# Between two layers of a decoder: weights rounded and turned in another order, two subtractions on GpSimd

## The chip, the cores and the metric

The kernel runs on one core of a Trainium2 chip. The metric is the device time of one execution in microseconds. Five engines work side by side: TensorE (PE; its weight loads are PEld), VectorE (DVE), ScalarE (ACT), GpSimd (POOL) and SyncE (SP), which here issues all DMAs. Each takes its own instructions in order and waits for others by semaphores.

## The reference, cut to what matters

256 tokens of width 1024 go through two layers, all in float32. Layer 0 is an HGRN2 mixer, layer 1 differential attention with one shared K/V; behind each mixer stands a grouped top-2 mixture of 16 experts. Each half of a layer ends in a residual sum and a normalisation:

```python
for l in range(DEPTH):                      # DEPTH = 2
    mix = hgrn2_mixer(x, ...) if l == 0 else diff_attention(x, k_sh, v_sh, ...)
    x = layer_norm(DEEPNORM_ALPHA * x + mix, ln1_g[l], ln1_b[l])
    ffn = moe_ffn(x, router_w, router_b, moe_w_gate[l], moe_w_up[l], moe_w_down[l])
    x = layer_norm(DEEPNORM_ALPHA * x + ffn, ln2_g[l], ln2_b[l])
```

Layer 1 begins with `x @ kv_w` and `x @ w_q`. The change lies between the end of the experts of layer 0 and these products.

## The kernel before, in words

**Products in three parts.** Activations and projection weights are split into a rounded high part and a low part (the rest). A projection is the sum of three products: high by high (number 0), the low part of x by the high weights (number 1), the high part of x by the low weights (number 2). The projection weights are cut into 36 pieces of 128 x 2048 (1 MB); `piece(i)` on TensorE multiplies one, in three groups of 16 products. `high(i)` on ScalarE (L805) rounds a piece into one of three buffers `w_hi`; `low(i)` on VectorE (L1185) subtracts that from the piece in place. `A_PIECES` is 20: pieces 0 to 19 belong to layer 0, piece 20 opens layer 1. The pieces lie in a ring of 12 places, which the expert weights use too; SyncE loads a place when the products that read it have ended. The buffers `w_hi` share memory with three of the four `spare` places of expert weights.

**Experts.** `moe(layer)` on each engine goes through 8 pairs of experts, two in each turn of a loop. In a pair TensorE multiplies gate (L2129), up (L2129), turns the hidden rows and multiplies down (L2143, L2160). ScalarE takes Silu (L1035), a copy of the hidden rows (L1039), and the output in two halves (`ys_hi`, L1052), of which VectorE takes the low part (L1667). After the last pair TensorE adds the outputs up (L2235) in four banks that hold the residual sum. An `overflow` part runs only if an expert has more tokens than its place holds; no instruction of it ran in the profiled execution. Behind it ScalarE loads the table with Ln and Exp (L1060), then runs `high(20)`.

**The passage between the layers.** VectorE takes the statistics of the four banks (L1674, L1214). ScalarE gives rstd by Ln (L859) and Exp (L862), VectorE refines it in small instructions (L1217 before, L1232 to L1236 after the root) and normalises token tile 0 (L1253), ScalarE tile 1 (L826), each in two halves. TensorE in the meantime multiplies zeros (`nothing`, L1850, 63 of them), then turns x by `turn_normed` (L1828 is the transpose) into four banks of PSUM: of a half, all four blocks of tile 0, then all of tile 1. From each bank the scaled and shifted x is written twice, rounded as `x_hi` and whole as `xT`: banks 0 and 2 by ScalarE (L819), 1 and 3 by VectorE (L1197); VectorE subtracts them into `x_lo` (L1728), and after each half it runs one `low`, of piece 20 or 21. Six more zero products of 256 columns (L2362) stand between the turns and piece 20. Piece 20 opens with the first product in two halves (L1895); all others come from L1906. `high(21)` follows ScalarE's part of this. GpSimd has nothing to do from its last weighing of gates (L756) to `affine` (L744), which scales and shifts the rows of x by two instructions of 128 x 2048.

**What sets the order.** It is written out by hand for each engine; nothing is planned at run time. A counting semaphore (`hi_ready`, `lo_ready`) says how many pieces are rounded and split; both are incremented in the order of the pieces.

Of the kernel before, what the change touches and what calls it, by code (L numbers as in the profile page):

```python
# [28 lines left out]
SLOTS = 64  # L29
# [62 lines left out]
def build(nc, ins, out):  # L92
    ctx = ExitStack()
    with ctx:
# [176 lines left out]
        o_gslot = sb("o_gslot", [P, 1])  # L271
        o_weights = [spare[:, c, :, :] for c in range(SPARE)] + late[1:3]

# [416 lines left out]
        def _(pool):  # L690
# [59 lines left out]
            for layer in range(LAYERS):  # L750
# [29 lines left out]

                if layer == 0:

                    pool.wait_ge(tp_ready, 4 * 2 + 4)
                    pool.wait_ge(kq_dve, 1)
                    affine()
# [8 lines left out]
        def _(act):  # L794
# [189 lines left out]
            def moe(layer):  # L984
                def overflow():
                    count = act.value_load(rounds[0:1, 0:1], min_val=1, max_val=ROUNDS)
                    with act.If(count > 1):
                        with act.Fori(1, count, 1):
                            act.wait_ge(orows_c_ps, done)
                            nc.scalar.activation(o_rows[:, 0:COLS], ps[:, BANK_C, :], ACT.Copy).then_inc(orows_act, 1)  # L990
                            act.wait_ge(oxc_ps, done)
                            for k in range(HALF_K):
# [16 lines left out]
                                                 scale=o_gslot[0:SLOTS, 0:1]).then_inc(oys_act, 1)  # L1009
                            act.reg_add(done, done, 1)  # L1010

                def take_xe(ready, value, bank, ks, cols):
# [17 lines left out]

                def experts(two, odd):
                    i = 2 * two + odd
                    pair = PAIRS * layer + i
                    act.wait_ge(gate_ps, 2 * pair + 2)
                    nc.scalar.activation(silu[:, :], ps[:, BANK_A, :], ACT.Silu).then_inc(silu_ready, 1)  # L1035
                    if not odd:
                        take_xe(xe_ps, gathered(layer, two, 0) + 1, BANK_C, (0, 1), slice(0, 4 * SLOTS))
                    act.wait_ge(ht_ps, pair + 1)
                    nc.scalar.activation(hT[:, :, :].rearrange("p j s -> p (j s)"), ps[:, BANK_A, :],  # L1039
                                         ACT.Copy).then_inc(ht_ready, 1)  # L1040
                    if not odd:
                        take_xe(xe_ps, gathered(layer, two, 0) + 2, BANK_B, (4, 5), slice(0, 4 * SLOTS))

                    act.wait_ge(put_ps, pair + 2)
                    nc.scalar.activation(silu[:, 0:T], ps[:, BANK_B if odd else BANK_A, 0:T], ACT.Copy,
                                         accum_out=gslot[:, 0:1]).then_inc(gslot_ready, 1)
                    for part, bank, ready in ((0, BANK_C, yc_ps), (1, BANK_D, yd_ps)):
                        act.wait_ge(ready, pair + 1)
                        if part == 0:
                            act.wait_ge(gslot_ready, pair + 1)  # L1050
                            act.wait_ge(seeded, TT * (layer + 1))
                        nc.scalar.activation(ys_hi[:, part * COLS:(part + 1) * COLS], ps[:, bank, :], ACT.Copy,  # L1052
                                             scale=gslot[:, 0:1]).then_inc(ys_act, 1)

                with act.Fori(0, PAIRS // 2, 1) as two:
                    experts(two, 0)
                    experts(two, 1)
                act.wait_ge(slots_ready, layer + 1)
                overflow()
                nc.scalar.preload_act_table_set(LOG_EXP)  # L1060
                if layer == 0:
                    high(A_PIECES)

# [23 lines left out]
            rounded_and_whole(2)  # L1087
            high(A_PIECES + 1)

# [79 lines left out]
        def _(dve):  # L1169
# [553 lines left out]
            for half in range(2):  # L1723
                rounded_and_whole(2 * half + 1)
                for ready, value in ((x_hi_ready, 5), (x_hi_dve, 5), (xT_act, 1), (xT_dve, 1)):
                    dve.wait_ge(ready, value + half)
                ks = slice(4 * half, 4 * half + 4)
                V.tensor_tensor(x_lo[:, ks, :], xT[:, ks, :], x_hi[:, ks, :].bitcast(F32), ALU.subtract  # L1728
                                ).then_inc(x_lo_ready, 1)
                low(20 + half)  # L1730

# [30 lines left out]
            def rms_of_sums(i, half, pairs):  # L1762
# [8 lines left out]
                step(rstd(i, values))  # L1771

            low(22)
            low(23)
# [48 lines left out]
        def _(pe):  # L1823
# [7 lines left out]
            def turn_normed():  # L1831
                for half in range(2):
                    for t in range(TT):
                        pe.wait_ge(x_half[t], half + 1)
                        for k in range(HALF_K * half, HALF_K * (half + 1)):
                            last = turn(x, t, k, TURN_BANKS[k // 2])
                            if t == 1 and k % 2:
                                last.then_inc(tp_ready, 1)

# [19 lines left out]
            def piece(i, after=()):  # L1859
# [15 lines left out]
                if (n, part) in ((AO1, 1), (BO1, 1)):  # L1875
# [6 lines left out]
                    return  # L1882
                for number, (w, xs) in enumerate(products):
                    if number == 1 and first_of_half:
# [422 lines left out]

            for _ in range(63):
                nothing(BANK_A, COLS // 4)
            turn_normed()  # L2310

# [48 lines left out]

            for _ in range(6):
                nothing(BANK_A, COLS // 2)  # L2362
            for i in range(20, 24):
# [40 lines left out]
```

## Time and profile before

| what | us |
|---|---|
| median of 3 runs (lowest, highest) | 700.84 (700.36, 702.13) |
| the profiled execution | 700.01 |
| its span, first to last instruction | 698.3 |
| TensorE busy in the span | 684.1 |
| VectorE, ScalarE, GpSimd busy | 307.1, 228.6, 52.8 |
| zero products between the layers begin | 354.60 |
| first turn of x, first product of piece 20 | 358.81, 361.18 |

Times inside the execution count from the first instruction. In the time-ordered views a row gives start, duration, engine, line of the kernel, operation, output and inputs, the count of instructions merged, and in brackets how long the engine had been idle before it and what released it. Two instructions of one engine can overlap by a tenth of a microsecond, since a record takes in the latency of its write.

### The profile page before, as it was taken

Reading aid. Unit: us, or ns where it says so; the run is one execution under the profiler, and the core shown is the slowest. Engines: PE = TensorE matmul, PEld = TensorE weight load, DVE = VectorE, ACT = ScalarE, POOL = GpSimd, SP = SyncE. Lnnn points to the kernel's source line nnn. Section 1 sums busy time; section 2 is a strip of 40 time slices with the busy share of each in tenths; the row PEclk is TensorE's granted clock in tenths of the full one; section 3 lists DMA queues with packets and bytes.
Section 4 is the critical chain, followed back from the end, with each engine's and each line's share of the span. In section 5 each row is a group of like instructions: output and inputs, shape, how many; then the busy total and the mean of one; then the engine's idle time right before and its main releaser. Section 6 shows DMA issues by size and latency. Waiting matters only on the chain.

```text
span 698.3 us, 13465 instructions
## 1 busy us (share of the span) xinstructions
PE 684.1 (98%) x5519; PEld 408.9 (59%) x5520; DVE 307.1 (44%) x563; ACT 228.6 (33%) x430; POOL 52.8 (8%) x57
## 2 busy tenths in 40 slices
PE   9999999999999999999999999999999999999993
PEld 8989988864335335335379987887433533533531
DVE  5689956686112012012076687678711111211205
ACT  4566567151112112012173656716111111211202
POOL 2035100010000000000004100001000000000001
PEclk9999999999999999999999999999999999999998
DMA  8999335989999999999999643498999999999991
GB/s 316 304 382 390 131 122 184 408 336 424 420 420 420 411 421 410 415 421 421 411 387 388 225 158 125 177 394 335 419 419 423 420 412 422 419 404 422 421 384 61
DMA packets 50870, 244.04 MB, mean 349 GB/s; under 512 B 6201, under 2 KB 6546, under 8 KB 26258
## 3 DMA queue, kind: packets, MB, share of 16 engines
q1 hardware_dynamic: 50834, 243.55, 87.3%
q8 instruction: 24, 0.39, 0.2%
q14 instruction: 12, 0.10, 0.0%
HBM read 242.49 MB, written 1.05 MB: 349 GB/s over the span
## 4 chain that ended last, share of the span: by engine, by line
PE 89%; DVE 7%; ACT 2%; issue 1%; ACTq 0%; DVEq 0%
PE ps L2129 32%; PE ps L1911 10%; PE ps L1906 10%; PE ps L2160 8%; PE ps L2143 8%; PE ps L2110 5%; PE ps L2091 4%; DVE ring_lo L1185 2%; PE ps L1878 2%; PE ps L1828 1%; PE ps L2099 1%; PE ps L2057 1%; PE ps L2197 1%; PE ps L1850 1%; DVE scratch L1343 1%
## 5 line engine op out<-in xcount | busy, mean ns | idle before, releaser
L2129 PE MATMUL ps<-weights,scratch 128*32 128x512 f32 (+1 forms) x1536 | 167.8, 592 | 0.0
L2129 PEld LDWEIGHTS ps<-weights,scratch 128*32 128x32 f32 x1536 | 49.9, 110 | 113.9 <-issue 113.9
L1185 DVE TENSOR_TENSOR ring_lo<-weights,w_hi 128x2048 fp32r<-128x2048 f32 x36 | 81.9, 2292 | 9.4 <-ACT w_hi L805 9.2
L1686 DVE TENSOR_TENSOR scratch<-ps,early 128x512 f32<-128x512 f32 x16 | 11.0, 689 | 168.1 <-PE ps L2129 168.1
L805 ACT ACTIVATE w_hi<-weights 128x2048 fp32r<-128x2048 f32 x35 | 66.6, 1914 | 22.9 <-PE ps L1911 11.5
L1667 DVE SCALAR_TENSOR_TENSOR rounded<-ps,gslot,rounded 128x512 fp32r<-128x512 f32 x32 | 24.0, 751 | 91.7 <-ACT rounded L1052 91.7
L2129 PE MATMUL ps<-tail,scratch 128*32 128x512 f32 (+1 forms) x512 | 56.4, 592 | 0.0
L1052 ACT ACTIVATE rounded<-ps,gslot 128x512 fp32r<-128x512 f32 x32 | 22.0, 688 | 88.4 <-PE ps L2160 47.0
L1017 ACT ACTIVATE scratch<-ps,ln_col 128x256 f32<-128x256 f32 (+1 forms) x40 | 19.3, 540 | 86.9 <-PE ps L2110 84.7
L1035 ACT ACTIVATE early<-ps 128x512 f32<-128x512 f32 x16 | 9.6, 597 | 98.7 <-PE ps L2129 98.7
L2129 PEld LDWEIGHTS ps<-tail,scratch 128*32 128x32 f32 x512 | 16.6, 110 | 38.3 <-issue 38.3
L1906 PE MATMUL ps<-x_lo,w_hi 128*128 128x256 f32 x256 | 33.8, 285 | 0.0
L756 POOL TENSOR_TENSOR early<-rounded,gate_of 128x256 f32<-128x256 f32 x14 | 8.6, 616 | 330.0 <-PE ps L2215 330.0
L1906 PE MATMUL ps<-x_hi,ring_lo 128*128 128x256 f32 x256 | 33.4, 283 | 0.0
L1639 DVE TENSOR_SCALAR scratch<-ps,ln_col 128x256 f32<-128x256 f32 (+1 forms) x40 | 18.7, 513 | 32.0 <-PE ps L2110 30.8
L2110 PE MATMUL ps<-rounded 128*128 128x256 f32 x128 | 32.2, 290 | 0.0
L1906 PEld LDWEIGHTS ps<-x_lo,w_hi 128*128 128x128 f32 x256 | 31.8, 191 | 0.5 <-issue 0.3
L1906 PEld LDWEIGHTS ps<-x_hi,ring_lo 128*128 128x128 f32 x256 | 31.8, 192 | 0.2 <-DVE ring_lo L1185 0.2
L2091 PE MATMUL ps<-rounded,early_r 128*128 128x512 f32 x112 | 31.5, 411 | 0.0
L2110 PE MATMUL ps<-rounded,x_lo 128*128 128x256 f32 x128 | 31.3, 283 | 0.0
L2160 PE MATMUL ps<-places,scratch 128*32 128x512 f32 (+1 forms) x256 | 30.6, 595 | 0.0
L2160 PE MATMUL ps<-weights,scratch 128*32 128x512 f32 (+1 forms) x256 | 30.4, 592 | 0.0
(293 smaller groups left out, 991.2 us busy)
## 6 DMA issues: line engine op xcount, KB each, us to landing
weights<-in_moe_w_gate SPq DMA_DIRECT2D x64, 1024.0 KB, 12.6
weights<-in_moe_w_up SPq DMA_DIRECT2D x32, 1024.0 KB, 11.5
places<-in_moe_w_down SPq DMA_DIRECT2D x32, 1024.0 KB, 11.1
tail<-in_moe_w_up SPq DMA_DIRECT2D x32, 1024.0 KB, 16.6
weights<-in_moe_w_down SPq DMA_DIRECT2D x32, 1024.0 KB, 11.2
weights<-in_a_w_in SPq DMA_DIRECT2D x15, 1024.0 KB, 12.9
weights<-in_kv_w SPq DMA_DIRECT2D x8, 1024.0 KB, 15.6
weights<-in_a_w_out SPq DMA_DIRECT2D x4, 1024.0 KB, 15.2
```

Of the source, the lines that this page charges most:

```text
L805: nc.scalar.activation(w_hi[:, i % HI, :, :].rearrange("p k n -> p (k n)"), ring[:, piece_slot(i), :, :].rearrange("p k n -> p (k n)"), AC ...
L1017: last = nc.scalar.activation(xe[:, k, cols], ps[:, bank, j * width:(j + 1) * width], ACT.Identity, scale=ln_col(2 * layer, 0, k), bias=ln ...
L1052: nc.scalar.activation(ys_hi[:, part * COLS:(part + 1) * COLS], ps[:, bank, :], ACT.Copy, scale=gslot[:, 0:1]).then_inc(ys_act, 1)
L1185: V.tensor_tensor(low_part(i), ring[:, piece_slot(i), :, :], w_hi[:, i % HI, :, :].bitcast(F32), ALU.subtract).then_inc(lo_ready, 1)
L1667: V.scalar_tensor_tensor(ys_lo[:, cols], ps[:, (BANK_C, BANK_D)[part], :], gslot[:, 0:1], ys_hi[:, cols].bitcast(F32), ALU.mult, ALU.subtr ...
L1906: last = mm(ps[:, bank, c * T:(c + 1) * T], w[:, k, first:first + P], xs[:, HALF_K * part + k, :], start=opens and c == 0 and k == 0, stop ...
L1911: last = mm(ps[:, bank, :], xs[:, HALF_K * part + k, j * P:(j + 1) * P], w[:, k, :], start=opens and k == 0, stop=closes and k == HALF_K - ...
L2091: last = mm(ps[:, 2 * t + j, :], put[:, t * P:(t + 1) * P], part[:, j * COLS:(j + 1) * COLS], start=False, stop=True, skip_group_check=True)
L2110: last = mm(ps[:, banks[j // 2], first:first + 4 * SLOTS], part[:, t, k * P:(k + 1) * P], pick[:, t, :, :].rearrange("p e s -> p (e s)"), ...
L2129: last = mm(ps[rows, bank, :], own[:, HALF_K * part + k, rows], w, start=part == 0 and k == 0, stop=part == 1 and k == HALF_K - 1)
L2143: last = mm(ps[rows, bank, :], hT[:, 2 * part + k, rows], w, start=part == 0 and k == 0, stop=part == 1 and k == 1)
L2160: last = mm(ps[rows, bank, :], hT[:, 2 * part + k, rows], w, start=part == 0 and k == 0, stop=part == 1 and k == 1)
```

## The change

In the experts' loop the last two pairs are written out behind it on ScalarE. The table with Ln and Exp is loaded right behind the last Silu, in both layers; in the overflow part the Silu table is loaded before and the other one after. In layer 0 `high(20)` stands between the two halves of the last pair's `ys_hi`, and `high(21)` behind the overflow part. The low parts of pieces 20 and 21 are made by GpSimd, behind its last weighing; VectorE's two are gone, and it waits for both before `low(22)`. The weights of the overflow part move to places that don't share memory with the buffers in use. `turn_normed` turns both tiles of a bank before it goes to the next. Piece 20 multiplies in the order 0, 2, 1. The 63 zero products of 128 columns become 40, with 29 of 64 columns behind them, and the six of 256 columns are gone.

```diff
--- before.py
+++ after.py
@@ -269,7 +269,7 @@
         o_hT = at(hid_place + F, FT, SLOTS)
         o_put = at(hid_place + F + FT * SLOTS, T)
         o_gslot = sb("o_gslot", [P, 1])
-        o_weights = [spare[:, c, :, :] for c in range(SPARE)] + late[1:3]
+        o_weights = [spare[:, c, :, :] for c in range(1, SPARE, 2)] + late[1:5]
 
         def o_weight(matrix, part):
             return o_weights[2 * matrix + part]
@@ -779,6 +779,10 @@
                 weigh(PAIRS // 2 - 1, 1)
 
                 if layer == 0:
+                    for i in range(A_PIECES, A_PIECES + 2):
+                        pool.wait_ge(hi_ready, i + 1)
+                        pool.tensor_tensor(low_part(i), ring[:, piece_slot(i), :, :], w_hi[:, i % HI, :, :].bitcast(F32),
+                                           ALU.subtract).then_inc(lo_ready, 1)
 
                     pool.wait_ge(tp_ready, 4 * 2 + 4)
                     pool.wait_ge(kq_dve, 1)
@@ -985,6 +989,7 @@
                 def overflow():
                     count = act.value_load(rounds[0:1, 0:1], min_val=1, max_val=ROUNDS)
                     with act.If(count > 1):
+                        nc.scalar.preload_act_table(ACT.Silu)
                         with act.Fori(1, count, 1):
                             act.wait_ge(orows_c_ps, done)
                             nc.scalar.activation(o_rows[:, 0:COLS], ps[:, BANK_C, :], ACT.Copy).then_inc(orows_act, 1)
@@ -1008,6 +1013,7 @@
                             nc.scalar.activation(o_ys[0:SLOTS, :], ps[0:SLOTS, BANK_A, :], ACT.Copy,
                                                  scale=o_gslot[0:SLOTS, 0:1]).then_inc(oys_act, 1)
                             act.reg_add(done, done, 1)
+                        nc.scalar.preload_act_table_set(LOG_EXP)
 
                 def take_xe(ready, value, bank, ks, cols):
 
@@ -1028,11 +1034,13 @@
                 take_xe(xc_ps, layer + 1, BANK_C, range(0, 4), columns_of(0))
                 nc.scalar.preload_act_table(ACT.Silu)
 
-                def experts(two, odd):
+                def experts(two, odd, last_pair=False):
                     i = 2 * two + odd
                     pair = PAIRS * layer + i
                     act.wait_ge(gate_ps, 2 * pair + 2)
                     nc.scalar.activation(silu[:, :], ps[:, BANK_A, :], ACT.Silu).then_inc(silu_ready, 1)
+                    if last_pair:
+                        nc.scalar.preload_act_table_set(LOG_EXP)
                     if not odd:
                         take_xe(xe_ps, gathered(layer, two, 0) + 1, BANK_C, (0, 1), slice(0, 4 * SLOTS))
                     act.wait_ge(ht_ps, pair + 1)
@@ -1051,15 +1059,18 @@
                             act.wait_ge(seeded, TT * (layer + 1))
                         nc.scalar.activation(ys_hi[:, part * COLS:(part + 1) * COLS], ps[:, bank, :], ACT.Copy,
                                              scale=gslot[:, 0:1]).then_inc(ys_act, 1)
-
-                with act.Fori(0, PAIRS // 2, 1) as two:
+                        if last_pair and part == layer == 0:
+                            high(A_PIECES)
+
+                with act.Fori(0, PAIRS // 2 - 1, 1) as two:
                     experts(two, 0)
                     experts(two, 1)
+                experts(PAIRS // 2 - 1, 0)
+                experts(PAIRS // 2 - 1, 1, last_pair=True)
                 act.wait_ge(slots_ready, layer + 1)
                 overflow()
-                nc.scalar.preload_act_table_set(LOG_EXP)
                 if layer == 0:
-                    high(A_PIECES)
+                    high(A_PIECES + 1)
 
             def second_parts(layer):
                 act.wait_ge(parts_ps, TT * layer + 2)
@@ -1085,7 +1096,6 @@
             normalise(1)
             rounded_and_whole(0)
             rounded_and_whole(2)
-            high(A_PIECES + 1)
 
             def take_kq(n):
                 dst = qT if n in (BQ0, BQ1) else kT
@@ -1727,7 +1737,6 @@
                 ks = slice(4 * half, 4 * half + 4)
                 V.tensor_tensor(x_lo[:, ks, :], xT[:, ks, :], x_hi[:, ks, :].bitcast(F32), ALU.subtract
                                 ).then_inc(x_lo_ready, 1)
-                low(20 + half)
 
             def take_kq(n):
                 dst = qT if n in (BQ0, BQ1) else kT
@@ -1770,6 +1779,7 @@
                 V.scalar_tensor_tensor(values(0), squares, 1.0 / P, low_end, ALU.mult, ALU.add).then_inc(var_ready, 1)
                 step(rstd(i, values))
 
+            dve.wait_ge(lo_ready, A_PIECES + 2)
             low(22)
             low(23)
             take_kq(K0)
@@ -1829,13 +1839,12 @@
                                            src[:, t, k * P:(k + 1) * P], ident[:, :])
 
             def turn_normed():
-                for half in range(2):
+                for pair in range(HALF_K):
                     for t in range(TT):
-                        pe.wait_ge(x_half[t], half + 1)
-                        for k in range(HALF_K * half, HALF_K * (half + 1)):
-                            last = turn(x, t, k, TURN_BANKS[k // 2])
-                            if t == 1 and k % 2:
-                                last.then_inc(tp_ready, 1)
+                        pe.wait_ge(x_half[t], pair // 2 + 1)
+                        for k in (2 * pair, 2 * pair + 1):
+                            last = turn(x, t, k, TURN_BANKS[pair])
+                    last.then_inc(tp_ready, 1)
 
             def turn_half(half, value):
                 for t in range(TT):
@@ -1880,7 +1889,8 @@
                         if number == 2 and k == HALF_K - 1:
                             last.then_inc(proj_ready, 1)
                     return
-                for number, (w, xs) in enumerate(products):
+                for number in (0, 2, 1) if i == A_PIECES else range(3):
+                    w, xs = products[number]
                     if number == 1 and first_of_half:
                         pe.wait_ge(x_lo_ready, 2 * call + part + 1)
                     if number == 2:
@@ -2305,8 +2315,10 @@
 
 
 
-            for _ in range(63):
+            for _ in range(40):
                 nothing(BANK_A, COLS // 4)
+            for _ in range(29):
+                mm(ps[:, BANK_A, 0:SLOTS], zeros16[:, :], zeros16[:, 0:SLOTS], start=True, stop=True)
             turn_normed()
 
             def attention_scores(h):
@@ -2358,8 +2370,6 @@
                         attention_out(h)
                 return between
 
-            for _ in range(6):
-                nothing(BANK_A, COLS // 2)
             for i in range(20, 24):
                 piece(i)
             piece(24, (attend(0),))
```

## Rows read from the trace of the kernel before

**Rows 1.** Page, part 1: busy us, share of the span, instructions

```profile
PE 684.1 (98%) x5519; PEld 408.9 (59%) x5520; DVE 307.1 (44%) x563; ACT 228.6 (33%) x430; POOL 52.8 (8%) x57
```

**Rows 2.** TensorE in order of time: start, us, what

```profile
354.60 3.75 PE L1850 MATMUL ps<-zeros 128*128 128x128 bf16 x63 [0.21 <-issue]
358.81 1.97 PE L1828 MATMUL ps<-ident,x_sb 128*128 128x128 f32 x16 [0.46 <-DVE x_sb L1253]
360.61 0.82 PE L1850 MATMUL ps<-zeros 128*128 128x256 bf16 x6
361.18 2.15 PE L1895 MATMUL ps<-x_hi,w_hi 128*128 128x256 f32 x16
...
367.46 2.08 PE L1906 MATMUL ps<-x_hi,w_hi 128*128 128x256 f32 x16
369.38 2.08 PE L1906 MATMUL ps<-x_lo,w_hi 128*128 128x256 f32 x16
...
684.55 2.40 PE L2235 MATMUL ps<-rounded,early_r 128*128 128x512 f32 x8
```

**Rows 3.** ScalarE in order of time, same stretch

```profile
348.69 0.69 ACT L1052 ACTIVATE rounded<-ps,gslot 128x512 fp32r<-128x512 f32 x1 [3.13 <-PE ps L2160]
...
353.49 1.28 ACT L1060 ACT_TABLE_LOAD   x1 [0.67 <-issue]
...
356.60 0.28 ACT L859 ACTIVATE rs<-mv,eps 128x2 f32<-128x2 f32 x1
...
359.72 1.02 ACT L819 ACTIVATE x_hi<-ps,pcol 128x256 fp32r<-128x256 f32 x2 [0.34 <-PE ps L1828]
```

**Rows 4.** VectorE in order of time, same stretch

```profile
356.03 0.28 DVE L1214 BATCH_NORM_AGGREGATE mv<-stats 128x2 f32<-128x12 f32 x2
...
357.22 0.35 DVE L1232 SCALAR_TENSOR_TENSOR rs<-rs 128x1 f32<-128x1 f32 x2 [0.70 <-ACT rs L862]
...
357.94 1.53 DVE L1253 TENSOR_SCALAR x_sb<-ps,mv,rs 128x512 f32<-128x512 f32 x2
...
361.97 1.23 DVE L1728 TENSOR_TENSOR x_lo<-xT,x_hi 128x1024 fp32r<-128x1024 f32 x1
...
375.70 2.29 DVE L1185 TENSOR_TENSOR ring_lo<-weights,w_hi 128x2048 fp32r<-128x2048 f32 x1
```

**Rows 5.** GpSimd in order of time, whole span

```profile
52.63 2.02 POOL L738 TENSOR_TENSOR scratch<-scratch 128x512 f32<-128x512 f32 x1 [11.66 <-ACT scratch L927]
...
65.97 1.30 POOL L738 TENSOR_TENSOR scratch<-scratch 128x512 f32<-128x512 f32 x1 [2.95 <-ACT scratch L927]
...
375.92 11.25 POOL L744 TENSOR_TENSOR x_sb<-x_sb,scratch 128x2048 f32<-128x2048 f32 x2 [53.61 <-DVE scratch L1190]
474.38 2.68 POOL L769 TENSOR_SCALAR scratch<-x_sb,mv,rs 128x512 f32<-128x512 f32 x1 [87.21 <-DVE rs L1236]
484.92 0.62 POOL L763 TENSOR_TENSOR early<-rounded,gate 128x256 f32<-128x256 f32 x1 [7.86 <-DVE scratch L1639]
```

**Rows 6.** VectorE in order of time, beside GpSimd and alone

```profile
53.59 1.60 DVE L1341 TENSOR_TENSOR scratch<-scratch 128x512 f32<-128x512 f32 x1
...
70.69 0.69 DVE L1341 TENSOR_TENSOR scratch<-scratch 128x512 f32<-128x512 f32 x1
...
485.08 0.47 DVE L1579 CAST second<-rg 1x7 int32<-1x7 f32 x1
```

**Rows 7.** DMA issues near 329.5 and 332, last column us to landing

```profile
weights<-in_kv_w SPq DMA_DIRECT2D x1, 1024.0 KB, 18.2
...
weights<-in_kv_w SPq DMA_DIRECT2D x1, 1024.0 KB, 20.5
```

**Rows 8.** TensorE in order of time, small bf16 products in layer 1

```profile
478.44 0.18 PE L2065 MATMUL ps<-both,later 128*128 128x16 bf16 x1
...
478.56 0.17 PE L2069 MATMUL ps<-both,ones 128*128 128x16 bf16 x1
```

**Rows 9.** Windows: stretch, length, busy times, granted clock, DMA share, GB/s

```profile
691.90:692.10 0.20, 0.00 (x0) 0.00 (x0) 0.20 (x1) 0.00 (x0) 0.20 (x1) 0.75 0.00 0
```

## What the change does to the time: the prediction

> **What bounds the kernel now.** I read the page first, then the chain of waits, which in the passage between the two layers runs through ScalarE's `high(20)` and logarithm, VectorE's small instructions and L1253 to the turns, then that stretch engine by engine in order of time, and last the places where GpSimd and VectorE read SBUF together. TensorE is busy for 684.1 of 698.3 us [rows 1], so every microsecond that it loses or wins between the layers moves the end; none of its waits is for a DMA, and the expert loops of the second layer are issued against its progress, so they shift with it. The passage is this. TensorE ends the experts and plays 63 zero products from 354.60; the last is over near 358.35. It then stands 0.46 us until VectorE has written the first normalised half, turns x at 358.81, plays six zero products at 360.61, and starts piece 20 at 361.18 [rows 2]. A group of sixteen products is followed by the next after 1.92 us (367.46 to 369.38), and a piece has three groups, 5.76 us; but piece 20 takes 6.28, from 361.18 to 367.46: its second group waits for x_lo, done at 363.20 (L1728, 361.97 and 1.23 [rows 4]), its third for the low part that VectorE makes behind that.
>
> What comes before the first turn is the normalisation's small work. The variance is there at 356.31 (356.03 and 0.28) [rows 4], but ScalarE is in `high(20)`, and the logarithm starts at 356.60 [rows 3]. The first of VectorE's five small instructions starts at 357.22, and L1253 follows at 357.94 [rows 4]: 0.72 us from first to next. The first turn starts 0.87 us behind L1253.
>
> **The change part by part.** The sum is against the profiled execution, 700.01 us (span 698.3); the median of the three runs is 0.83 higher, 700.84.
>
> *Rounding and table on ScalarE.* The table load (1.28 us at 353.49 [rows 3]) goes behind the last Silu, in front of ScalarE's wait for the up products and the turned hidden rows: no cost. In layer 1 it stood before a wait for VectorE anyway: no gain. `high(20)` goes behind ScalarE's first half of the last outputs, which ends at 349.38; its weights were issued at 329.53 and took 18.2 us, so they are there at 347.7 [rows 3, 7]. It runs to about 351.3, and the second half still starts at 352.13. `high(21)` takes the table load's place: its load is issued by 332.4 and lands 20.5 us later, 352.9 at the latest [rows 7]; it runs from 353.5 to 355.4. So the logarithm follows the variance at once, near 356.35 instead of 356.60: -0.24 us, if nothing else is late. The peeled pair costs some straight-line code beside long waits, which I take as nothing.
>
> *Turns and zero products.* Turning bank by bank lets ScalarE start after 4 turns instead of 6, 0.24 us earlier (16 turns run 1.80 us, 0.11 each, from 358.81 to 360.61 [rows 2]). That matters only because the six zero products go: ScalarE's x_hi (359.72 and 1.02 [rows 3]) is ready 1.93 us after the first turn, with the change 1.69, and the turns last 1.80. The first product then follows the turns directly: -0.57 us (361.18 less 360.61). The filler ahead: 40 products of 128 columns at 57 ns (3.75 us less one 0.22 latency, over 62) are 2.3 us. For 29 of 64 columns there is no row; five of 16 columns follow each other at about 28 ns (478.44 to 478.56 for the first and fifth [rows 8]), 128 columns at 57; so 0.8 to 1.7 us, and I take 0.9, nearer the small ones. The filler then ends by 357.9, at worst at 358.6, when the first turn could not start sooner than 358.57: nothing to 0.1 us.
>
> *Order (0, 2, 1) and the low parts on GpSimd.* Piece 20 no longer waits for VectorE's low part, and x_lo, ready 4.4 us after the first turn (361.97 and 1.23 against 358.81 [rows 2, 4]), is asked for 5.6 us after it (1.80 and two groups of 1.92). Both stalls go: 6.28 less 5.76, -0.52 us. VectorE is freed of two subtractions of 2.29 us (the length of L1185 [rows 4]), which no later product waits for. Together, from the first turn on: 0.57 + 0.52 = 1.09 us won.
>
> *What GpSimd does to VectorE.* This is where the change turns round. GpSimd takes 9.2 us for two instructions of the same size (375.92 and 11.25 give 387.17; it could not begin before VectorE's L1185, 375.70 and 2.29, was over at 377.99) [rows 4, 5]: 4.6 us each. From 65.97 one of 512 elements takes 1.30, four times that is 5.2, the upper bound; I take 4.6, the same shape. `low(20)` starts 0.1 us behind `high(20)`, at 351.4, and ends at 356.0. `low(21)` has its input since 355.4 and follows: 356.05 to 360.65. Ready in time for TensorE, both. But while a two-input GpSimd instruction runs, a VectorE instruction that reads two tensors in SBUF stands still. L1341 takes 1.60 us at 53.59 and 0.69 at 70.69; it ends at 55.19, half a microsecond after GpSimd's L738 (52.63 and 2.02, so 54.65) [rows 5, 6]. Size doesn't save it: a cast of 1x7 at 485.08 takes 0.47 us and ends at 485.55, where GpSimd's L763 (484.92 and 0.62) ends at 485.54 [rows 5, 6]. L1232, L1234, L1235 and L1236 read two SBUF tensors each, and the first of them would be issued at 357.0, a microsecond into `low(21)`. It stands until 360.65. The chain to L1253 is 0.72 us from there, or 0.57 since the standing instruction's own start is over; L1253 starts at about 361.3 instead of 357.94: +3.36 us. This takes in the 0.24 that ScalarE had won. Queued behind L1232 on VectorE is all of the normalisation, ScalarE's half of it, and with them the turns, so TensorE, too. L1217 (before L1232, one input) may be held as well: up to +0.25.
>
> Sum: 3.36 - 1.09 = +2.27 us, 702.3 against 700.01, or 703.1 against the median.
>
> [...]
>
> **The rivals.**
> A. *GpSimd's reads don't hold these small instructions.* For it: L769 holds nothing, and no row shows a 128x1 operand under a two-input GpSimd instruction. Against it: the 1x7 cast. Then all the gains stand: 0.24 + 1.09 = 1.33 us, 698.7 in the profile, 699.5 by the median, not slower. The same comes if `low(21)` starts only after L1236, that is later than about 357.7; it would need the second weights to land 3 us later than the bound above. It decides at one point: whether GpSimd is in a two-input instruction when L1232 is issued.
> B. *The held time also costs the clock.* TensorE stands from 357.9 to 362.2, 4.3 us. At the end of the span its last product ends at 686.95 (684.55 and 2.40 [rows 2]) and the granted clock goes from 1.00 to 0.50, to 1.2 GHz, at 692.0 (0.75 in 691.9 to 692.1 [rows 9]), 5.05 us later. So 4.3 us is a little short of what that drop took. If it falls here, at least the turns take twice their 1.80 us, and perhaps the first group of products, 1.92, too: 1.8 to 3.7 more. Total +4.1 to +6.0: 704.9 to 706.8.
> C. *GpSimd is slower for this output type* (it never writes rounded values before). At the bound of 5.2 us each `low(21)` ends at 361.85: +1.2, so 704.3.
>
> **How the numbers follow.** Held, clock kept, GpSimd at 4.6: 0.62, time 703.1, own range 702.7 to 703.7. Held and slower (C): 0.08. Held and clock lost (B): 0.16. Not held (A): 0.14. The range from 701.2 to 705.6 leaves out A and the far end of B. A measurement tells 0.3%, 2.1 us, from no change. The forecast of +2.3 lies just over it: of the 0.70 in the held cases at full clock about 0.17 falls within 2.1, with nearly all of A the chance of no difference is 0.29; slower 0.67; faster 0.04.
>
> **What would show it.** VectorE's L1232 between the layers lasts about 3.7 us and ends with GpSimd's second subtraction; ScalarE's logarithm starts near 356.35; TensorE's first turn starts near 362.2, its first piece 1.8 us later, pieces 20 and 21 take 5.76 us each without a stall. A first turn before 359, with GpSimd at work beside it, would prove the main step wrong; a granted clock of 0.50 behind the wait would show B; GpSimd's subtractions longer than 4.8 us would show C.

## The result and the profile after

The change makes the kernel slower: 704.20 us median (703.57 to 705.62, 7 runs) against 700.84 (7 runs beside it). The ratio is 1.0053, with a 95% interval of 1.0044 to 1.0062. The profiled execution took 704.20 us with a span of 702.5; that is 4.2 us more span than before. The forecast was slower, 703.1.

In the kernel after, lines stand lower: L1850 is now L1859 (its 64-column form L2321), L1828 is L1838, L1895 and L1906 are L1905 and L1916, L1217 is L1227, L1232 is L1242, L1253 is L1263. The kernels of the experiments shift them again by a few lines: L1217 is L1229 in e1 and e11, L1232 in e7, L1233 in e12.

TensorE of the kernel after, in order of time, answers to [rows 2]:

```profile
354.50 2.47 PE L1859 MATMUL ps<-zeros 128*128 128x128 bf16 x40 [0.21 <-issue]
356.81 1.01 PE L2321 MATMUL ps<-zeros 128*128 128x64 bf16 x29
361.86 3.68 PE L1838 MATMUL ps<-ident,x_sb 128*128 128x128 f32 x16 [4.04 <-DVE x_sb L1263]
365.19 3.22 PE L1905 MATMUL ps<-x_hi,w_hi 128*128 128x256 f32 x16
368.24 2.08 PE L1916 MATMUL ps<-x_hi,ring_lo 128*128 128x256 f32 x16
...
372.08 2.08 PE L1916 MATMUL ps<-x_hi,w_hi 128*128 128x256 f32 x16
...
688.75 2.40 PE L2245 MATMUL ps<-rounded,early_r 128*128 128x512 f32 x8
```

The first turn waits 4.04 us, and sixteen turns then last 3.33 us until the next group instead of 1.80. VectorE, the same stretch ([rows 4]):

```profile
355.94 0.28 DVE L1224 BATCH_NORM_AGGREGATE mv<-stats 128x2 f32<-128x12 f32 x2
356.25 3.98 DVE L1227 TENSOR_SCALAR rs<-mv 128x2 f32<-128x2 f32 x1
360.26 0.35 DVE L1242 SCALAR_TENSOR_TENSOR rs<-rs 128x1 f32<-128x1 f32 x2
...
360.99 1.53 DVE L1263 TENSOR_SCALAR x_sb<-ps,mv,rs 128x512 f32<-128x512 f32 x2
```

GpSimd and ScalarE, the same stretch, each in order of time ([rows 3] has ScalarE's before):

```profile
351.16 9.04 POOL L784 TENSOR_TENSOR ring_lo<-weights,w_hi 128x2048 fp32r<-128x2048 f32 x2 [28.95 <-ACT w_hi L809]
```

```profile
353.05 1.92 ACT L809 ACTIVATE w_hi<-weights 128x2048 fp32r<-128x2048 f32 x1 [0.33 <-issue]
356.25 0.29 ACT L863 ACTIVATE rs<-mv,eps 128x2 f32<-128x2 f32 x1 [1.29 <-DVE mv L1224]
```

An instruction on two numbers per partition takes 3.98 us, and ends (360.23) with GpSimd's second subtraction (351.16 + 9.04 = 360.20). The windows of the kernel after have the granted clock in the third column from the right:

```profile
358.00:360.00 2.00, 0.00 (x0) 0.00 (x0) 2.00 (x1) 0.00 (x0) 2.00 (x1) 1.00 1.07 391
360.00:362.00 2.00, 0.14 (x1) 0.14 (x2) 1.90 (x8) 1.01 (x2) 0.20 (x1) 0.69 1.04 384
362.00:364.00 2.00, 2.00 (x10) 2.00 (x11) 0.65 (x2) 1.43 (x4) 0.00 (x0) 0.50 1.05 385
364.00:366.00 2.00, 2.00 (x12) 2.00 (x11) 1.87 (x5) 2.00 (x6) 0.00 (x0) 0.50 1.06 393
366.00:368.00 2.00, 2.00 (x12) 2.00 (x12) 2.00 (x4) 2.00 (x3) 0.00 (x0) 0.60 1.04 408
368.00:372.00 4.00, 4.00 (x36) 4.00 (x35) 3.87 (x5) 0.57 (x1) 0.00 (x0) 1.00 1.04 389
```

TensorE has been idle since 357.82. A mean of 0.69 over two microseconds puts the step from 1.00 to 0.50 (2.4 to 1.2 GHz) at 360.8, and 0.60 puts the step back at 367.6. The turns and most of the first group of products ran at half clock.

**Where the 4.2 us are.** I count from the start of the zero products, since that is the same work in every kernel: so what a profiled execution gains or loses ahead of the passage drops out (the zeros start anywhere from 354.50 to 356.54 in the kernels below).

| us from the start of the zeros | before | after | e1 | e2 |
|---|---|---|---|---|
| first turn | 4.21 | 7.36 | 3.98 | 7.37 |
| first turn to first product | 2.37 | 3.33 | 1.86 | 1.86 |
| piece 20 | 6.28 | 6.89 | 5.82 | 5.82 |
| in all: piece 21 begins | 12.86 | 17.58 | 11.66 | 15.05 |

e1 is the change without the hold (`low(21)` later), e2 the change with the hold but with TensorE kept busy. So the edits that were to gain give 12.86 - 11.66 = 1.20; the hold costs 15.05 - 11.66 = 3.39; the lost clock costs 17.58 - 15.05 = 2.53. Together +4.72. The passage begins 0.10 earlier (354.50 against 354.60), so piece 21 begins 4.62 later; 0.4 us come back at 441, where a wait of TensorE is gone (below), and the last group of products starts 4.20 later, at 688.75 instead of 684.55.

### The profile page after: what moved, and what is told of

Read it like the earlier page. It is cut to its first block, busy times and chain, and to the rows that moved or that the text cites. A ratio compares the mean times of both kernels' runs of the same rounds, so it can differ in the third digit from the quotient of the medians.

```text
span 702.5 us, 13451 instructions
## 1 busy us (share of the span) xinstructions
PE 685.1 (98%) x5519; PEld 410.5 (58%) x5520; DVE 310.0 (44%) x561; ACT 228.8 (33%) x430; POOL 62.0 (9%) x59
## 4 chain that ended last, share of the span: by engine, by line
PE 95%; DVE 3%; ACT 1%; issue 0%; DVEq 0%; ACTq 0%
PE ps L2139 31%; PE ps L1921 14%; PE ps L1916 13%; PE ps L2170 8%; PE ps L2153 8%; PE ps L2120 5%; PE ps L2101 4%; PE ps L1887 2%; PE ps L1838 1%; PE ps L2109 1%; PE ps L2067 1%; PE ps L2207 1%; PE ps L1859 1%; PE ps L1905 1%; DVE stats L1684 1%; DVE rs L1227 1%
## 5 line engine op out<-in xcount | busy, mean ns | idle before, releaser
L1916 PE MATMUL ps<-x_lo,w_hi 128*128 128x256 f32 x256 | 33.7, 284 | 0.0
L1916 PE MATMUL ps<-x_hi,ring_lo 128*128 128x256 f32 x256 | 33.3, 283 | 0.0
L1916 PEld LDWEIGHTS ps<-x_lo,w_hi 128*128 128x128 f32 x256 | 31.8, 191 | 0.3 <-issue 0.3
L1916 PEld LDWEIGHTS ps<-x_hi,ring_lo 128*128 128x128 f32 x256 | 31.9, 192 | 0.0
```

The source lines that it names most:

```text
L1916: last = mm(ps[:, bank, c * T:(c + 1) * T], w[:, k, first:first + P], xs[:, HALF_K * part + k, :], start=opens and c == 0 and k == 0, stop ...
```

## The experiments

All ratios are against the kernel before, run on the same chip. Most differences are small against 700 us, so the column "piece 21 begins", counted from the zeros as above, is read first and the time second. It comes from one profiled execution of each kernel; e1, e9, e10 and e13, which do the same work there, agree in it within 0.01, as do before and e5.

| kernel | median us (runs) | ratio, 95% interval | piece 21 begins, us |
|---|---|---|---|
| e1_after_stat | 698.62 (7) | 0.9973, 0.9962 to 0.9984 | 11.66 |
| e2_long_filler | 703.04 (6) | 1.0033, 1.0021 to 1.0045 | 15.05 |
| e3_lows_on_vector | 700.39 (10) | 0.9998, 0.9988 to 1.0007 | 12.65 |
| e5_no_six_zeros | 700.74 (10) | 1.0003, 0.9994 to 1.0012 | 12.87 |
| e6_order_012 | 700.62 (10) | 1.0000, 0.9990 to 1.0009 | 12.87 |
| e8_six_zeros_back | 699.88 (10) | 0.9986, 0.9977 to 0.9995 | 12.20 |
| e9_table_back | 699.52 (10) | 0.9982, 0.9973 to 0.9992 | 11.66 |
| e7_one_input | 706.45 (2) | 1.0080, 1.0061 to 1.0098 | 17.78 |
| e11_behind_l1217 | 706.39 (4) | 1.0072, 1.0055 to 1.0089 | 17.20 |
| e12_one_input_l1232 | 704.75 (2) | 1.0051, 1.0031 to 1.0072 | 16.33 |
| e10_vector_code | 698.99 (11) | 0.9973, 0.9964 to 0.9982 | 11.67 |
| e13_one_memset | 700.13 (10) | 0.9978, 0.9968 to 0.9988 | 11.66 |

**e1_after_stat.** `low(21)` on GpSimd starts only when VectorE's small instructions are over.

```diff
+                        if i > A_PIECES:
+                            pool.wait_ge(ln_stat, 2)
```

> The changed kernel with one wait more: GpSimd starts its subtraction for piece 21 only when VectorE has finished the statistics (ln_stat 2). Theory (VectorE is held by GpSimd's two-input instruction, and the wait that follows costs TensorE its clock): both go, the first turn starts near 358.5 instead of 361.86, piece 20 starts 1.8 us later, the clock stays at 1.00; 1.3 us faster than the kernel before, ratio 0.998. Rival (the loss comes from the filler, the peeled pair on ScalarE or the order of turns): the first turn stays near 361.9 and the time near 704.

Measured: 698.62, and the interval of the ratio excludes 1. TensorE, VectorE and GpSimd of this kernel, each in order of time:

```profile
354.64 2.41 PE L1861 MATMUL ps<-zeros 128*128 128x128 bf16 x40 [0.21 <-issue]
...
358.62 1.97 PE L1840 MATMUL ps<-ident,x_sb 128*128 128x128 f32 x16 [0.73 <-DVE x_sb L1265]
360.48 2.14 PE L1907 MATMUL ps<-x_hi,w_hi 128*128 128x256 f32 x16
...
366.30 2.08 PE L1918 MATMUL ps<-x_hi,w_hi 128*128 128x256 f32 x16
```

```profile
356.40 0.17 DVE L1229 TENSOR_SCALAR rs<-mv 128x2 f32<-128x2 f32 x1
357.03 0.35 DVE L1244 SCALAR_TENSOR_TENSOR rs<-rs 128x1 f32<-128x1 f32 x2 [0.46 <-ACT rs L868]
...
361.79 1.72 DVE L1740 TENSOR_TENSOR x_lo<-xT,x_hi 128x1024 fp32r<-128x1024 f32 x1
```

```profile
351.31 4.57 POOL L786 TENSOR_TENSOR ring_lo<-weights,w_hi 128x2048 fp32r<-128x2048 f32 x1 [28.96 <-ACT w_hi L811]
357.86 4.57 POOL L786 TENSOR_TENSOR ring_lo<-weights,w_hi 128x2048 fp32r<-128x2048 f32 x1 [1.98 <-DVE rs L1248]
```

The same 128x2 instruction takes 0.17 us when GpSimd is idle beside it, against 3.98. One wait moves the kernel from slower to faster, so the hold, with the clock that it costs, is the whole loss. `x_lo` now meets `low(21)` and is held 0.5 us (1.72 against 1.23 [rows 4]), which in the order 0, 2, 1 nobody waits for. VectorE's four L1209 behind L1265, which read PSUM, keep their length beside it (0.99 to 1.00 us for two, as L1207 in the changed kernel without it). This version is faster than both kernels.

**e2_long_filler.** 66 more zero products, to fill the held time.

```diff
-            for _ in range(40):
+            for _ in range(106):
```

> The changed kernel with 106 instead of 40 zero products of 128 columns, so that TensorE is busy until about 361.6 while VectorE is held. Theory (hold and clock are two costs): the hold stays, first turn near 361.9, but the clock stays at 1.00 and 2.6 us come back: about +2.0 us against the kernel before (702.8), 1.4 to 2.7 faster than the changed kernel. Rival (the slow turns and first products come from something else than the idle time): no gain, near 704.2.

TensorE of this kernel, and one window with its granted clock:

```profile
354.81 6.15 PE L1859 MATMUL ps<-zeros 128*128 128x128 bf16 x106 [0.20 <-issue]
360.80 1.01 PE L2321 MATMUL ps<-zeros 128*128 128x64 bf16 x29
362.18 1.97 PE L1838 MATMUL ps<-ident,x_sb 128*128 128x128 f32 x16 [0.38 <-DVE x_sb L1263]
364.04 2.14 PE L1905 MATMUL ps<-x_hi,w_hi 128*128 128x256 f32 x16
...
369.86 2.08 PE L1916 MATMUL ps<-x_hi,w_hi 128*128 128x256 f32 x16
```

```profile
361.00:364.00 3.00, 2.62 (x44) 2.41 (x40) 2.46 (x7) 2.57 (x5) 0.00 (x0) 1.00 1.05 388
```

The hold stays (first turn at 7.37 as at 7.36), the clock does not fall, and 2.53 us of the passage go. In the medians it is less: 704.20 less 703.04 is 1.2 us, the ratios differ by 0.0020 and their intervals just touch; of e2 the profiled execution (702.18) is the fastest of six. The mean granted clock of the whole execution says that the clock is lost in every run of the change: 0.990 to 0.992 in its seven, 0.993 to 0.995 in the six of e2. How many microseconds of it other executions pay, no trace shows.

**e3_lows_on_vector.** The GpSimd part undone: both low parts back on VectorE, order 0, 1, 2 again; the rest of the change stays.

```diff
-                    for i in range(A_PIECES, A_PIECES + 2):
-                        pool.wait_ge(hi_ready, i + 1)
-                        pool.tensor_tensor(low_part(i), ...)
...
+                low(20 + half)
...
-                for number in (0, 2, 1) if i == A_PIECES else range(3):
+                for number in range(3):
```

> The changed kernel with GpSimd's part alone undone: the low parts of pieces 20 and 21 are VectorE's again, after each half of x_lo, and piece 20 multiplies in the order 0, 1, 2. Theory: no hold and no lost clock; the logarithm is 0.24 us earlier and the zero products are gone, but piece 20 then stands longer for x_lo and its low part, which are ready only 0.24 us earlier than before: -0.3 us against the kernel before. Rival (the six zero products cost their full 0.57 us wherever VectorE stands): -0.8 us.

Measured: no change in the time, and 0.21 in the passage. TensorE has this:

```profile
359.33 1.97 PE L1834 MATMUL ps<-ident,x_sb 128*128 128x128 f32 x16 [0.67 <-DVE x_sb L1259]
361.19 2.15 PE L1901 MATMUL ps<-x_hi,w_hi 128*128 128x256 f32 x16
363.78 2.18 PE L1912 MATMUL ps<-x_lo,w_hi 128*128 128x256 f32 x16 [0.44 <-DVE x_lo L1734]
```

The product starts right behind the turns, and then its half microsecond is spent again in front of x_lo. What remains is the earlier logarithm.

**e5_no_six_zeros.** The kernel before, without the six zero products alone.

```diff
-            for _ in range(6):
-                nothing(BANK_A, COLS // 2)
```

> The kernel before with nothing but the six zero products of 256 columns left out. Theory: piece 20 starts 0.4 us earlier (x_hi ready at 360.74), but its third group still waits for VectorE's low part at 365.4: no change, within 0.1 us. Rival: the time falls by 0.4 to 0.6 us.

Measured: nothing, 12.87 against 12.86. The first product starts 2.08 us after the first turn instead of 2.37; the gain is lost at x_lo, for which TensorE stands 0.22 us. The six zeros of the kernel before stood where TensorE would have waited anyway.

**e6_order_012** and **e8_six_zeros_back.** e1 with the old order, and e1 with the six zeros.

```diff
-                for number in (0, 2, 1) if i == A_PIECES else range(3):
+                for number in range(3):
```

```diff
+            for _ in range(6):
+                nothing(BANK_A, COLS // 2)
```

> e1_after_stat with piece 20 in the order 0, 1, 2. Theory: its second group then waits for x_lo, ready 4.9 us after the first turn (GpSimd holds it half a microsecond) and asked for 3.8 after it: +1.1 us, near 699.7. Rival (x_lo is never late): no change.

> e1_after_stat with the six zero products of 256 columns put back between the turns and piece 20. Theory (piece 20 is now bound by TensorE alone): they cost their 0.57 us in full, 699.2, where leaving them out of the kernel before brought nothing. Rival (something else holds piece 20): no change against e1_after_stat.

TensorE and VectorE of e6:

```profile
360.88 2.14 PE L1907 MATMUL ps<-x_hi,w_hi 128*128 128x256 f32 x16
363.99 2.18 PE L1918 MATMUL ps<-x_lo,w_hi 128*128 128x256 f32 x16 [0.96 <-DVE x_lo L1740]
```

```profile
362.19 1.74 DVE L1740 TENSOR_TENSOR x_lo<-xT,x_hi 128x1024 fp32r<-128x1024 f32 x1
```

In the old order TensorE waits 0.96 us for an x_lo that GpSimd holds; 12.87 less 11.66 is 1.21, all that e1 gains. Half a microsecond of this is the hold of x_lo, so it is the price of the old order beside GpSimd and not of the order alone. In e8 the six zeros cost 12.20 - 11.66 = 0.54. The order with GpSimd's low parts pays even with the six zeros in place (piece 20 takes 5.84 us in e8, from 361.75 to 367.59, for 6.28); dropping the zeros pays only with these two (e5, e3). The new order with VectorE's low parts was not run.

**e9_table_back.** e1 with the table load behind the overflow part, where it was.

```diff
-                    if last_pair:
-                        nc.scalar.preload_act_table_set(LOG_EXP)
...
                 overflow()
+                nc.scalar.preload_act_table_set(LOG_EXP)
```

> e1_after_stat with the table load back behind the overflow part, ahead of the rounding of piece 21. Theory: rounding then ends near 356.6, after the variance at 356.36, the logarithm starts 0.2 to 0.3 us later and so does everything behind it: +0.25 us. Rival (ScalarE has room for it): no change in the start of the logarithm.

ScalarE of this kernel:

```profile
354.86 1.28 ACT L1072 ACT_TABLE_LOAD   x1 [0.24 <-issue]
356.15 1.91 ACT L811 ACTIVATE w_hi<-weights 128x2048 fp32r<-128x2048 f32 x1
358.15 0.29 ACT L865 ACTIVATE rs<-mv,eps 128x2 f32<-128x2 f32 x1
```

Piece 21 begins at 11.66, as in e1. The rounding ends (358.06) just when the variance comes (358.11), so the logarithm starts no later than in e1 and the expected 0.25 us are not there. Moving the table is worth nothing once one of the two roundings has been moved. The median lies 0.9 us above e1's; that comes from elsewhere (last experiment).

**Which instructions are held.** Three kernels put GpSimd beside other instructions. e11: `low(21)` starts right behind L1217 and so meets L1232. e7: a one-input instruction of GpSimd (the whole piece by 1.0) stands directly behind `low(20)` and meets L1217. e12: the same instruction starts behind L1217 and meets L1232. In e7 and e12 `low(21)` waits for the statistics as in e1.

```diff
+                            pool.wait_ge(lam_exp_ready, 3)     # e11, e12: counted up behind L1217
+                            pool.tensor_scalar(w_hi[:, 1, :, :], ring[:, piece_slot(i), :, :], 1.0, None,
+                                               ALU.mult).then_inc(lam_exp_ready, 1)      # e7, e12
```

> The changed kernel with GpSimd's subtraction for piece 21 started when L1217 (TENSOR_SCALAR, one input) is done, at about 356.6, so that it meets VectorE's two-input instructions on 128x1 and 128x2 (L1232 to L1236) and not L1217, which in the changed kernel was held first and hid them. Theory (a two-input GpSimd instruction holds two-input VectorE instructions whatever their size): L1232 stands until 361.1, the first turn starts near 362.2, time 702.5 to 705. Rival (only L1217 was held, the small two-input ones are not): first turn near 358.6, time as with the wait for the statistics, 698.7.

> e1_after_stat with a GpSimd tensor_scalar of 128 x 2048, one input in SBUF, put directly behind the subtraction for piece 20, where that for piece 21 had stood; it writes a free buffer, and ScalarE waits for it before it rounds piece 22. Theory by the rows (L769 beside VectorE's small two-input instructions): a one-input GpSimd instruction holds nothing, the first turn stays near 358.6, the time within 0.3 us of e1_after_stat. Rival, the rule of the Trainium skill (SBUF - State Buffer, Who interferes with whom: a VectorE instruction with two SBUF inputs contends with any GpSimd instruction that reads SBUF): VectorE stands from 357.0 until it ends, at 358 to 361 by its length (at L769's rate of 5.2 ns an element even longer).

> e1_after_stat with a one-input GpSimd tensor_scalar of 128 x 2048 started when L1217 is done (5.4 us, to about 362.0), the subtraction for piece 21 behind it. e7_one_input has shown that such an instruction holds L1217. Theory by the rows beside L769: it does not hold the two-input L1232 to L1236, the first turn stays near 358.6, time within 0.5 us of e1_after_stat. Rival by the Trainium skill's rule (SBUF - State Buffer, Who interferes with whom: two SBUF inputs contend with any GpSimd instruction that reads SBUF): VectorE stands until 362.0 and the first turn starts near 363.0.

VectorE and GpSimd of e11, of e7 and of e12, a fence for each engine:

```profile
358.30 0.17 DVE L1229 TENSOR_SCALAR rs<-mv 128x2 f32<-128x2 f32 x1
358.86 4.46 DVE L1246 SCALAR_TENSOR_TENSOR rs<-rs 128x1 f32<-128x1 f32 x2 [0.39 <-ACT rs L868]
```

```profile
358.67 4.50 POOL L786 TENSOR_TENSOR ring_lo<-weights,w_hi 128x2048 fp32r<-128x2048 f32 x1 [0.89 <-DVEq L1231]
```

```profile
358.29 4.97 DVE L1232 TENSOR_SCALAR rs<-mv 128x2 f32<-128x2 f32 x1
```

```profile
357.86 5.38 POOL L785 TENSOR_SCALAR w_hi<-weights 128x2048 fp32r<-128x2048 f32 x1
```

```profile
358.05 3.62 DVE L1250 SCALAR_TENSOR_TENSOR rs<-rs 128x1 f32<-128x1 f32 x2 [0.40 <-ACT rs L871]
```

```profile
357.87 5.38 POOL L786 TENSOR_SCALAR w_hi<-weights 128x2048 fp32r<-128x2048 f32 x1 [0.90 <-DVEq L1235]
```

e11: the two 128x1 instructions take 4.46 us instead of 0.35 and end 0.15 after GpSimd. So two-input instructions are held down to one element per partition, as the prediction had it; L1217 only stood in front of them. e7: I had read L769 [rows 5] as a sign that a one-input instruction of GpSimd holds nothing. It held L1217 to its end (358.29 and 4.97 give 363.26; GpSimd ends at 363.24). e12: it held the two-input pair too, but let it go after 3.62 us, 1.6 us before its own end at 363.25, and the three two-input instructions behind the pair then ran beside it at their usual 0.15 to 0.16 us. So neither "holds nothing" nor "holds to the end" is right there. Why L769 held nothing and this one let go early stays open.

**The 0.4 us at 441.** The chain of waits of the kernel before has a gap there, on VectorE ahead of L1770:

```profile
438.97 0.43 issue
439.40 0.18 DVE rs L1770
```

TensorE waits some 2 us further on:

```profile
441.71 1.09 PE L1828 MATMUL ps<-ident,scratch 128*128 128x128 f32 x8 [0.53 <-ACT scratch L1103]
```

The gap's place in the kernel after, where TensorE starts the same eight turns at 445.93 without a wait:

```profile
443.56 0.05 issue
443.62 0.18 DVE rs L1779
```

It is 0.43 in before, e3 and e5, and 0.05 in every kernel whose low parts lie on GpSimd. e10 lengthens e1's VectorE stream with a wait and two memsets, and the profile counts 563 instructions on it, as in before [rows 1]; e13 has one memset more than e1 (562 counted), which by its expectation makes the stream equal to before's with the waits taken in.

```diff
             dve.wait_ge(lo_ready, A_PIECES + 2)
+            dve.wait_ge(hi_ready, A_PIECES + 2)    # e10 only
+            V.memset(lam[:, 6:7], 0.0)             # e10 only
+            V.memset(lam[:, 7:8], 0.0)
             low(22)
```

> e1_after_stat with two memsets of one column (of a small tile that nothing reads) and one wait more on VectorE, ahead of its subtraction for piece 22, so that its instruction stream is as long as before. The new kernels lack a stall of 0.38 us that before has at 441 us, where VectorE's L1770 starts 0.43 us after its release without waiting for anything. Theory (it hangs on where the instruction lies in the stream of VectorE): the stall comes back, first turn and pieces 20, 21 as in e1_after_stat, +0.4 us. Rival (it went because VectorE has less work or because the stage comes earlier): it stays away, time as e1_after_stat.

> e1_after_stat with one memset of one column on VectorE ahead of its subtraction for piece 22: its stream then has exactly as many instructions as before, where e10_vector_code had one more. Theory (the 0.43 us at L1770 hang on the place in the stream, to the instruction): the stall near 440 comes back, +0.4 us. Rival: it stays away again.

In both the gap stays at 0.05, so a stream of the old length by either count does not bring it back. What makes it is open.

e13's median lies 1.5 us above e1's, though the intervals of their ratios overlap and the passage is the same. Its trace has 1.3 us of that in front of two small products behind the choice of experts, one in each layer, where e1's TensorE does not stand:

```profile
147.00 0.18 PE L2078 MATMUL ps<-both,later 128*128 128x16 bf16 x1 [0.67 <-DVE both L1569]
...
478.80 0.18 PE L2078 MATMUL ps<-both,later 128*128 128x16 bf16 x1 [0.66 <-DVE both L1569]
```

The traces of e7, e9 and e12 have both waits and that of e11 the second, each 0.66 to 0.69 us long; before, the change and the other experiments have neither. So the medians of these four and of e13, as far as one trace of each tells, carry some 0.7 to 1.4 us that do not come from the passage. Why is open.

## Why the prediction was right, and where it was off

**The main step held.** Slower was forecast because GpSimd's reads would stand between VectorE and its small instructions until `low(21)` ends. The two subtractions took 4.52 us each for my 4.6 and began 0.2 us earlier than I had them, so they ended at 360.20, not 360.65. The hold was to cost 3.36 + 0.24 = 3.60 us, the logarithm's gain within it; it costs 3.39 (e2 less e1).

**The first instruction held was another.** The prediction named L1232 as the one that stands, and gave L1217 up to 0.25 us as a possibility. L1217 stood for 3.98 us, and ScalarE's root and VectorE's wait for it passed unseen beside it. L1232 would have been next: e11 shows it. The price hardly differs: L1263 follows GpSimd's end by 0.79 us in the change (360.99 less 360.20), and by 0.52 where L1232 is the one that stands (e11, 363.69 less 363.17), so 0.27 us more. The totals of the two can't be compared so: in e11 the hold costs 4.04 us (first turn 8.02 us from the zeros, 3.98 in e1), since GpSimd starts later there, and the clock 1.50. The Trainium skill (VectorE: DVE Perf Modes, "Mode 2×_2P") says that a float32 tensor_scalar from SBUF to SBUF may use both of VectorE's read ports for its one input; with the rule on such modes in SBUF — State Buffer, "Who interferes with whom", that would hold L1217. The trace agrees, 3.98 us in place of 0.17; whether L1217 ran in that mode, no run shows. The prediction went by the count of inputs, though its own row for small sizes was against that: the 1x7 cast of [rows 6] has one input too and ends with GpSimd's instruction, and a 1x8 cast with no GpSimd beside it (L1598 at 488.42) takes 0.16 us for its 0.47.

**The gains.** Worked out: 0.24 + 0.57 + 0.52 = 1.33. In e1's trace: the first turn 0.23 earlier, first turn to first product 0.51 less, piece 20 0.46 less, together 1.20. The first product starts 1.86 us after the first turn, 0.06 later than the turns' 1.80, and its group takes 1.98 for 1.92. Both terms stand about as sized, but not as equals: the 0.52 of the order and the low parts comes without the other too (e8, 0.44), while the 0.57 of the zeros is there only because these have taken the waits for x_lo and the low part away (e5, e3).

**The term left out of the sum: the clock.** Rival B is what happened. The forecast had the clock kept, and B, its loss, at a chance of 0.16, because the idle time (4.3 us forecast, 4.04 measured) was shorter than the 5.05 us from the last product to the fall at the end of the span [rows 2, 9]. One such pair bounds nothing: here it fell 2.9 us after the last product. The cost was worked out as 1.8 to 3.7 and is 2.53. With that term the sum would have been 3.36 - 1.09 + 2.53 = +4.8, and the time by the median 705.6, the edge of the range. That the median of 704.20 lies well inside it, 1.1 us from the 703.1 of a case that did not occur, is in part luck: 0.4 us came back at 441, which no term had, the hold was 0.2 smaller, and the profiled execution of before was 0.83 below its median where that of the change equals its own, so that the medians rose by 3.4 us and the profiled executions by 4.2. Rivals A and C fall: the small instructions were held, and GpSimd was not slower.

**What was not foreseen** is the 0.4 us that come back at 441.

## What to carry to other kernels

Work moved to an idle GpSimd may hold any instruction of VectorE that reads SBUF: look at which VectorE instruction is *issued* while GpSimd runs, however small it is, and price it with the rest of GpSimd's instruction. Not every such pair collides (L769, and the end of e12), so it has to be measured. Here one wait on a semaphore that already existed turned the change from 1.0053 to 0.9973. A stall of some microseconds in front of TensorE is priced twice, once as idle time and once as the clock that it may cost; and dropping idle work ahead of a wait pays only once the wait behind it is gone.

## What the runs showed of the hardware

- One input on each side is enough: GpSimd's tensor_scalar held VectorE's 128x2 tensor_scalar for 4.97 us (e7). GpSimd took 5.38 us for 128x2048 with one input and 4.5 to 4.6 with two.
- What VectorE read from PSUM was not held: its four statistics instructions (L1684, L1674 before, 128x512) take 2.48 us beside GpSimd's first subtraction, as without it.
- The granted clock fell at no fixed distance from the last product. Read from the 2 us stretches: 2.9 us after it in the kernel after, 2.2 in e7, 4.7 in e12 and 5.2 in e11. In the last two TensorE was at work again when it fell, 0.9 and 0.5 us before. The windows of e11 (work since 364.56) and e12 (since 362.90) in which it fell, in this order; in the next 2 us both have 0.50:

```profile
364.00:366.00 2.00, 1.44 (x9) 1.45 (x10) 1.22 (x2) 1.83 (x4) 0.00 (x0) 0.76 1.06 388
```

```profile
362.00:364.00 2.00, 1.10 (x9) 1.10 (x10) 1.53 (x3) 1.85 (x3) 2.00 (x2) 0.94 1.05 389
```
